# A SwiGLU block's down projection: 22 accumulating row blocks, or seven block products in sequence

## The reference

```python
x = x + rms_norm(mixed, g_post_mix)
h2 = rms_norm(x, g_pre_ffn)
ff = (jax.nn.silu(h2 @ w_gate) * (h2 @ w_up)) @ w_down
return x + rms_norm(ff, g_post_ffn)
```

## Time and profile before

| | us |
|---|---|
| median of 3 runs (605.81 to 607.92) | 607.17 |
| the profiled execution | 606.58 |
| its span, first to last instruction | 604.9 |
| TensorE busy | 589.1 (97%) |
| VectorE busy | 419.2 (69%) |
| ScalarE busy | 287.9 (48%) |
| GpSimd busy | 97.3 (16%) |

### The profile page before, as it was taken

How to read it: one execution, slowest core, us unless ns; L and a number is a source line. 1 busy time by engine, 2 the same in 40 slices (tenths; PEclk the granted TensorE clock), 3 DMA queues, 4 the chain that set the end, 5 groups by cost and what they waited for, 6 DMA issues and landing times.

```text
span 604.9 us, 9970 instructions
## 1 busy us (share of the span) xinstructions
PE 589.1 (97%) x3588; PEld 522.7 (86%) x3588; DVE 419.2 (69%) x704; ACT 287.9 (48%) x503; POOL 97.3 (16%) x98
## 2 busy tenths in 40 slices
PE   4999999999999999989999999999999999999996
PEld 4778888888888788989999999999999988888885
DVE  3768888787767955689887888788878632334433
ACT  6636665666535653545535353535353433224322
POOL 1111000010000000283332323232321100000000
PEclk9999999999999999999999999999999999999999
DMA  7644333333123550301313231323132473332111
GB/s 285 174 147 111 110 122 90 121 104 105 42 89 115 172 211 35 140 2 70 140 71 139 78 130 69 139 77 131 69 139 84 142 296 104 104 100 74 36 69 69
DMA packets 19540, 68.15 MB, mean 113 GB/s; under 512 B 2827, under 2 KB 2827, under 8 KB 19512
## 3 DMA queue, kind: packets, MB, share of 16 engines
q1 hardware_dynamic: 15944, 55.70, 26.4%
q0 software_dynamic: 3568, 12.09, 6.8%
HBM read 60.41 MB, written 4.22 MB: 107 GB/s over the span
## 4 chain that ended last, share of the span: by engine, by line
PE 91%; DVE 5%; ACT 1%; issue 1%; DMA 1%; SPq 0%; DVEq 0%; ACTq 0%
PE bank L1318 16%; PE bank L1320 16%; PE bank L1319 16%; PE bank L1568 11%; PE bank L1569 11%; PE bank L1570 11%; PE bank L1450 2%; PE bank L1438 2%; PE bank L1356 2%; PE bank L1422 1%; PE bank L1420 1%; DMA x_sb<-in_x 1%; DVE tok_lo L1228 1%; DVE form_lo L1152 1%; DVE mix_y L1130 1%
## 5 line engine op out<-in xcount | busy, mean ns | idle before, releaser
L1568 PE MATMUL bank<-tok_hi,form_hi 128*128 128x256 f32 x320 | 90.6, 283 | 0.4 <-DVE sp_v L1198 0.4
L1570 PE MATMUL bank<-tok_hi,form_lo 128*128 128x256 f32 x320 | 90.6, 283 | 0.0
L1569 PE MATMUL bank<-tok_lo,form_hi 128*128 128x256 f32 x320 | 90.6, 283 | 0.0
L889 DVE TENSOR_TENSOR w_lo<-raw,w_hi 128x1024 fp32r<-128x1024 f32 x46 | 55.7, 1218 | 43.0 <-ACT w_hi L574 42.9
L1318 PE MATMUL bank<-hn_hi,w_hi 128*128 128x512 f32 (+2 forms) x200 | 80.5, 403 | 0.0
L1320 PE MATMUL bank<-hn_hi,w_lo 128*128 128x512 f32 (+2 forms) x200 | 77.2, 386 | 0.0
L1319 PE MATMUL bank<-hn_lo,w_hi 128*128 128x512 f32 (+2 forms) x200 | 76.7, 384 | 0.0
L574 ACT CAST w_hi<-raw 128x1024 fp32r<-128x1024 f32 x46 | 47.9, 1046 | 48.1 <-PE bank L1320 45.6
L1569 PE MATMUL bank<-hn_lo,form_hi 128*128 128x256 f32 x240 | 67.9, 283 | 0.0
L1570 PE MATMUL bank<-hn_hi,form_lo 128*128 128x256 f32 x240 | 67.9, 283 | 0.0
L1568 PE MATMUL bank<-hn_hi,form_hi 128*128 128x256 f32 x240 | 67.9, 283 | 0.0
(11 more groups left out here) (195 smaller groups left out, 1329.6 us busy)
## 6 DMA issues: line engine op xcount, KB each, us to landing
raw<-in_w_in_units SPq DMA_DIRECT2D x24, 512.0 KB, 3.3
raw<-in_w_gate_units SPq DMA_DIRECT2D x22, 512.0 KB, 3.3
raw<-in_w_up_units SPq DMA_DIRECT2D x22, 512.0 KB, 4.2
raw<-in_w_down SPq DMA_DIRECT2D x22, 512.0 KB, 3.3
raw<-in_w_out SPq DMA_DIRECT2D x8, 512.0 KB, 3.3
q_lh<-q_hl POOLq DMA_DIRECT2D x12, 256.0 KB, 2.8
x_sb<-in_x SPq DMA_DIRECT2D x4, 512.0 KB, 5.1
x_rows<-x_sb POOLq DMA_DIRECT2D x4, 512.0 KB, 2.9
```

Source lines behind the costliest of these rows:

```text
L889: nc.vector.tensor_tensor(lo[:, :, :], raw[u % RAW][:, :, :], hi[:, :, :], ALU.subtract).then_inc(lo_done, 1)
L1568: nc.tensor.matmul(out_ap, sh, mh, start=first and k == 0, stop=False, skip_group_check=True)
L1569: nc.tensor.matmul(out_ap, sh, ml, start=False, stop=False, skip_group_check=True)
L1570: mm = nc.tensor.matmul(out_ap, sl, mh, start=False, stop=k == HK - 1, skip_group_check=True)
```

## The change

The down projection is done as seven products on 2 x 2 blocks as well. The activation is cut into two halves of features (11 blocks of 128 each) and two of tokens, `w_down` into two halves of rows and two of columns. Each of the seven products has 11 feature blocks x 2 token tiles x 3 matmuls of 512 columns. They run one after the other, with three pairs of PSUM banks (A, B, C) for the partial results.

The weight operand of a product is a block of `w_down` or a running sum of blocks. It is held in two places, `down_x` and `down_y` (22 KB a partition each), and its sums are made by transfers that add what they read to what lies in SBUF (`accum_op=ALU.add`), issued by GpSimd: block after block into `down_x` (products 1, 2 and 6) and `down_y` (product 4). SyncE loads `down_x` for product 0, `down_y` for product 3, and `down_y` again for product 5. Each of them comes in six groups of one or two row blocks (`DOWN_GROUPS`). The add of a group waits for the splitting of that group for the product that used it before.

The activation operand of products 0, 5 and 6 is a quarter of `act`; that of products 1 to 4 is a sum or difference of quarters in `down_s`, made by GpSimd in one instruction of 128 x 2816 numbers each (`down_sums`). ScalarE and VectorE split each operand whole (`down_form_hi`, `down_form_lo`, 128 x 2816) and the weights by groups (`down_hi`, `down_lo`) into four slots (`DSLOTS`); a slot is free when TensorE has finished the group four before. The join of partial results is done by ScalarE (`keep`, a copy out of PSUM) and VectorE (`join`). The norm at the end works on halves of a token tile. The diff, cut to this:

```diff
-LOOP_DOWN = 16
-LAST = FT - LOOP_DOWN
+DK = FT // 2
+DOWN_PRODUCTS = 7
+DOWN_GROUPS = ((3, 5), (5, 7), (7, 9), (9, 11), (0, 2), (2, 3))
+DG = len(DOWN_GROUPS)
+DOWN_SPLITS = DOWN_PRODUCTS * DG
+DSLOTS = 4
+DOWN_CHAIN = ((A_BANK, True), (C_BANK, True), (A_BANK, False), (C_BANK, False), (A_BANK, False), (B_BANK, True),
+              (A_BANK, False))
+DOWN_SOURCE = (("x", "in", 1), ("x", "added", 1), ("x", "added", 2), ("y", "in", 1), ("y", "added", 1), ("y", "in", 2),
+               ("x", "added", 3))
...
 @block.sync
+            for g in range(DG):
+                if g % 2 == 0 and g < 4:
+                    sp.wait_ge(form_lo_done, 4 * (SP_PAIRS - 1 + g // 2))
+                if g == 4:
+                    sp.wait_ge(prod, 7 * SP_PAIRS)
+                load_down("x", 0, 0, g)
+            for g in range(DG):
+                load_down("y", 1, 1, g)
+            for g in range(DG):
+                sp.wait_ge(dw_lo_done, DG * 4 + g + 1)
+                load_down("y", 1, 0, g)
...
 @block.gpsimd
             pool.wait_ge(act_done, FT)
             pool.dma_start(g_post_ffn_b[:, :], g_post_ffn.partition_broadcast(P)).then_inc(g_ffn_in, 16)
-            pool.wait_ge(prod, 7 * SP_PAIRS)
+            def add_down(which, f_half, n_half, n, g):
+                k0, k1 = DOWN_GROUPS[g]
+                dst = (down_x, down_y)[which == "y"]
+                pool.wait_ge(dw_lo_done, DG * n + g + 1)
+                pool.dma_start(dst[:, k0:k1, :], down_block(f_half, n_half, g), accum_op=ALU.add
+                               ).then_inc(down_added[which][g], 16)
+            def down_sums(n):
+                a11, a12 = act[:, 0:DK, 0:HALF], act[:, DK:FT, 0:HALF]
+                a21, a22 = act[:, 0:DK, HALF:SEQ], act[:, DK:FT, HALF:SEQ]
+                if n >= 2:
+                    pool.wait_ge(down_sum, n - 1)
+                    pool.wait_ge(da_lo_done, n)
+                else:
+                    pool.wait_ge(act_done, FT)
+                in0, in1, op = {1: (a21, a22, ALU.subtract), 2: (down_s[:, :, :], a11, ALU.subtract),
+                                3: (down_s[:, :, :], a12, ALU.add), 4: (a11, a21, ALU.subtract)}[n]
+                nc.gpsimd.tensor_tensor(down_s[:, :, :], in0, in1, op).then_inc(down_sum, 1)
+            down_sums(1)
+            for g in range(DG):
+                add_down("x", 0, 1, 0, g)
+            down_sums(2)
+            for g in range(DG):
+                add_down("x", 1, 1, 1, g)
+            down_sums(3)
+            for g in range(DG):
+                add_down("x", 1, 0, 2, g)
+            down_sums(4)
+            for g in range(DG):
+                add_down("y", 0, 1, 3, g)
+            pool.wait_ge(dw_lo_done, DG * 6)
...
 @block.scalar
+            def down_hi(s):
+                src, sem_in, count = down_raw(s)
+                act_e.wait_ge(sem_in, count)
+                if s >= DSLOTS:
+                    act_e.wait_ge(dw_used, s - DSLOTS + 1)
+                k0, k1 = DOWN_GROUPS[s % DG]
+                nc.scalar.copy(dw_hi[s % DSLOTS][:, 0:k1 - k0, :], src).then_inc(dw_hi_done, 1)
+            def down_form_hi(n):
+                if 1 <= n <= 4:
+                    act_e.wait_ge(down_sum, n)
+                if n >= 2:
+                    act_e.wait_ge(dw_used, DG * (n - 1))
+                nc.scalar.copy(da_hi[n % 2][:, :, :], down_form(n)).then_inc(da_hi_done, 1)
...
 turn(LAST_Q, ...), ScalarE
                     act_e.wait_ge(prod, 7 * LAST_Q)
-                    split(U_DOWN)
-                    split(U_DOWN + 1)
...
+                    down_form_hi(0)
                     act_e.wait_ge(form_lo_done, 4 * SP_PAIRS)
-                    for f in range(2):
-                        act_split(f, f)
+                    down_hi(0)
                 silu_first(q, par)
...
             silu_second(LAST_Q, LAST_Q % 2)
+            down_hi(1)
             act_e.wait_ge(prod, 7 * SP_PAIRS)
+            for s in range(2, DOWN_SPLITS):
+                down_hi(s)
+                if s % DG == 3 and s // DG + 1 < DOWN_PRODUCTS:
+                    down_form_hi(s // DG + 1)
+                if s in keep_at:
+                    keep(*keep_at[s])
...
 turn(LAST_Q, ...), VectorE
-                    split(U_DOWN)
-                    split(U_DOWN + 1)
                 if before:
                     product_of(q - 1, 1 - par)
                 sum_v6(q, par)
...
-                    act_split(0, 0, 1)
+                    down_form_lo(0)
                 sum_v67(q, par)
...
-                    act_split(1, 1, 2)
+                    down_lo(0)
                 up_second(q, par)
...
             gate_second(LAST_Q, LAST_Q % 2)
             product_of(LAST_Q, LAST_Q % 2)
+            down_lo(1)
+            for s in range(2, DOWN_SPLITS):
+                n, g = divmod(s, DG)
+                down_lo(s)
+                if g == 4:
+                    if n + 1 < DOWN_PRODUCTS:
+                        down_form_lo(n + 1)
+                    if n == 4:
+                        join(3, c12, True, ALU.subtract, 3)
+                    if n == 5:
+                        join(4, c22, False, ALU.subtract, 2)
+            join(5, c11, True, ALU.add, 1)
...
 @block.tensor
+            for n in range(DOWN_PRODUCTS):
+                pe.wait_ge(da_lo_done, n + 1)
+                if 2 <= n <= 4:
+                    pe.wait_ge(kept, n - 1)
...
+                if n == 6:
+                    pe.wait_ge(joined, 2)
+                for g in range(DG):
+                    if n == DOWN_PRODUCTS - 1 and g >= TAIL_GROUP:
+                        break
+                    pe.wait_ge(dw_lo_done, DG * n + g + 1)
+                    down_group(n, g, range(2)).then_inc(dw_used, 1)
+            for t in range(2):
+                for g in range(TAIL_GROUP, DG):
+                    if t == 0:
+                        pe.wait_ge(dw_lo_done, DG * (DOWN_PRODUCTS - 1) + g + 1)
+                    mm = down_group(DOWN_PRODUCTS - 1, g, (t,))
+                mm.then_inc(down_tile, 1)
```

More of the change, by code:

```diff
@@ L86 @@
 GU_BANKS = ((6, 7), (2, 3))
-DOWN_BANKS = (0, 4, 6, 2)
 STEPS = 8 * PAIRS
@@ L365, in norm_no, with down_block, down_raw, down_form @@
             return {SQ1: t + 1, SQ2: TT + 2 * t + 1, SQ3: TT + 2 * t + 2, SQ4: 3 * TT + t + 1}[n]
-        def nth(u):
-            return u + 1 if u < U_DOWN else u + 1 - 2 * SP_PAIRS
+        def down_block(f_half, n_half, g):
+            k0, k1 = DOWN_GROUPS[g]
+            return w_down[P * (DK * f_half + k0):P * (DK * f_half + k1),
+                          SEQ * n_half:SEQ * (n_half + 1)].rearrange("(k p) n -> p k n", p=P)
+        def down_raw(s):
+            n, g = divmod(s, DG)
+            which, by, count = DOWN_SOURCE[n]
+            k0, k1 = DOWN_GROUPS[g]
+            return ((down_x, down_y)[which == "y"][:, k0:k1, :], (down_in if by == "in" else down_added)[which][g],
+                    16 * count)
+        def down_form(n):
+            first, second = slice(0, HALF), slice(HALF, SEQ)
+            if n == 0:
+                return act[:, 0:DK, first]
+            if n == 5:
+                return act[:, DK:FT, first]
+            if n == 6:
+                return act[:, DK:FT, second]
+            return down_s[:, :, :]
         def raw_count(q):
@@ L883, in _ @@
+            act_e.wait_ge(joined, 3)
+            for t in range(2):
+                second_half(4 + t, t, 0, c11[:, t, :])
+            for t in range(2):
+                act_e.wait_ge(down_tile, t + 1)
+                second_half(6 + t, 2 + t, 0, bank[:, A_BANK + t, :])
         @block.vector
@@ L1614, in _ @@
                     pair(i * 2 + par, par)
-            def down(units, acts, t, first, last, halves=range(2)):
-                for h in halves:
-                    c = slice(4 * h, 4 * h + 4)
-                    mm = product(bank[:, DOWN_BANKS[t] + h, :],
-                                 (acts[0][:, P * t:P * (t + 1)], acts[1][:, P * t:P * (t + 1)]),
-                                 (units[0][:, c, :].rearrange("p k n -> p (k n)"),
-                                  units[1][:, c, :].rearrange("p k n -> p (k n)")), first, last)
-                return mm
@@ L1627, in _, with down_mm @@
[L1627 to L1637 removed]
+            def down_mm(n, k, slot, j, t, first, last):
+                b = DOWN_CHAIN[n][0]
+                (sh, sl), (mh, ml) = (da_hi[n % 2], da_lo[n % 2]), (dw_hi[slot], dw_lo[slot])
+                tokens_of = slice(P * t, P * (t + 1))
+                out_ap = bank[:, b + t, :]
+                nc.tensor.matmul(out_ap, sh[:, k, tokens_of], mh[:, j, :], start=first and DOWN_CHAIN[n][1],
+                                 stop=False, skip_group_check=True)
+                nc.tensor.matmul(out_ap, sh[:, k, tokens_of], ml[:, j, :], start=False, stop=False,
+                                 skip_group_check=True)
+                return nc.tensor.matmul(out_ap, sl[:, k, tokens_of], mh[:, j, :], start=False, stop=last,
```

(1 more changed line is left out.)

275 lines of the change are left out of this document (127 added, 148 removed).

## The result

| | before | after |
|---|---|---|
| median of the runs side by side | 606.71 (605.81 to 607.92) | 616.74 (608.73 to 617.79) |
| ratio, with its 95% interval | | 1.0134 [1.0084, 1.0184] |
| the profiled execution | 606.58 | 616.02 |
| its span | 604.9 | 614.3 |

The changed kernel is slower by 1.3%, where 604.8 us and a gain of 0.4% were forecast; 616.74 is inside the range of 600 to 632. Its own runs spread over 9 us, those of the kernel before over 2. Ten further runs of it (e0) had a median of 609.73, and all 14 together 612.1; so it is 2.5 to 10 us slower than the kernel before, depending on the set of runs, and none of the 14 reached the forecast (the fastest took 606.63).

A forecast was written before the change was run, and what follows sets the result against it. TensorE was taken as the bound, busy 97% of the span with nothing waiting. 15.0 us gained less 12.6 given back leaves 2.4: 607.17 to 604.8 us; 8-in-10 range 600 to 632.

The forecast's parts named there:

- The gain: Down projection: 462 matmuls in place of 528, 66 fewer at 0.2267 us each, saving 15.0 us.
- Parts 1 and 2: Last turn before the down projection loses 1.0 us; product 0 waits 0.3 us for group 1 and 4.8 for group 2.
- one or two us hang on the order of two engines: Product 0: if VectorE were just ahead of GpSimd, group 3 would be late, by some 3 us, instead of group 2.
- Part 3: Products 1, 2 and 3: a loop through GpSimd, ScalarE and VectorE outlasts TensorE's work, costing 3.6, 1.0 and 1.0 us.
- group 0 of the next product 1.14, which gets in before GpSimd's next sum: Products 1 to 3: VectorE's 1.14 us subtraction of the next product's group 0 precedes GpSimd's sum, which waits for group 5.
- The cycle: Each product with a sum: sum, casts and subtractions in a loop take 16.0 us with signalling, against TensorE's 14.96.
- Part 4: Weight transfers: only the last group of product 4 shows as waiting, 0.9 us, zero if adds are cheap.
- twice: Adding transfers cost twice a copy, both addends being read: 15.2 us an operand.
- 8 us of lead: Weight adds for a product are issued 8 us or more before ScalarE wants them.
- Part 5: Copies, joins and end: work lies in slack, steps behind the last matmul stay 5.5 us; cost 0, at most 1.
- The scaling of token tiles 0 and 1 has product 6 to hide it: Norm at the end: some 6 us of VectorE scaling fits within the 15 us of product 6.
- adding transfers too slow: Rival: below about 190 GB/s of added data an operand lands slower than 14.96 us; chance 0.42, two thirds above 615.

The follow-up runs named there:

- e6: Changed kernel with its 24 adding weight transfers made plain loads of the same number and size (output differs): 606.28 us, ratio 0.9996.
- e5: Changed kernel without the activation sums, products 1 to 4 taking plain quarters of `act` (output differs), adding transfers kept: 603.45 us, ratio 0.9944.
- e11: e9 with `down_y` loads waiting for product 2's splits and product 6's adds issued behind product 5's splits: 595.72 us, ratio 0.9806.
- e3: Changed kernel with 54 filler matmuls into an unused bank before TensorE's long waits, two semaphore waits moved to product 0: 613.57 us, ratio 1.0092.
- e7: Kernel before the change, with TensorE made to wait once in the tail for a GpSimd sum of 2048 numbers a partition: 613.48 us, ratio 1.0112.
- e2: Changed kernel with the norm's squares and the last join moved earlier, into product 6's loops: 610.58 us, ratio 0.9998.
- e9: Changed kernel with the edits of e1 and e2 together, transfers not moved: 598.54 us, ratio 0.9870.
- e1: Changed kernel with the four activation sums made by VectorE, not GpSimd: 602.28 us, ratio 0.9921.
- e4: Changed kernel with each GpSimd sum waiting until VectorE has done one more weight subtraction: 611.9 us, ratio 1.0083.
- e8: e9 with `down_y` loads waiting for product 1's splits and product 6's adds issued behind product 4's: 602.98 us, ratio 0.9945.
- e10: Changed kernel with each GpSimd sum cut into four instructions of 3, 3, 3 and 2 blocks: 617.40 us, ratio 1.0192.

## Why the prediction was wrong

Two steps turn the forecast gain of 2.4 us into a loss in the profiled execution: the waits were priced without the slower clock behind them (5.8 us), and the norm's work was held to be hidden (4.1 us). By parts:

**The gain** was right: 462 matmuls, 14.96 us a product.

**Parts 1 and 2** were right within 0.3 us. The long GpSimd instruction held VectorE whole, as rows 6 had shown for short ones, and a small fixed time plus a share proportional to size carried over from 1.29 to 6.55 us. That one or two us hang on the order of two engines was real, but at the start of product 1 and not in product 0: 1.5 us of waiting between e0's trace and the first one.

**Part 3** was right in product 1 (3.5 for 3.6) by luck, as another group was late for another reason, and too low by 3 us in products 2 and 3. The step that failed there is "group 0 of the next product 1.14, which gets in before GpSimd's next sum". In the profiled execution GpSimd got the ports first each time, so group 0 itself was held. The cycle had counted the cast of group 0 as ready; in product 1 it waited for the added weights and in product 2 for a slot. With plain loads (e6) it was ready, the order was the forecast one, and products 2 and 3 lost 0.7 us each (forecast 1.0). Product 1 lost 1.0 there, not 3.6; an estimate of the reason is the 2.7 us that half clock had cost TensorE in product 0 of e6, in which the weights caught up.

**Part 4**: "twice" was right (206 against 381 to 392 GB/s), its place was wrong. I let it cost 0.9 us in product 4; it cost nothing there and some 3.5 to 6 us in all (e6), by bringing group 0 so late that it met the sum, and it was the next limit once the sums were gone (e5). I had counted 8 us of lead for an add. Its landing took 9.8 us in the median, not the 3.3 of a lone load. Only part of that is `down_y`'s first load on the same engines, which I had named and not priced: with that load moved away (e11) the median is still 9.2, and with plain transfers (e6) it is 7.1.

**The clock** is the largest miss, 5.8 us, and no step of the prediction has it. Every wait in parts 2 and 3 was priced at its length alone. The page of the kernel before shows 1.00 throughout, because nothing there is idle; a change that brings idle stretches in leaves that state. e3 (idle time filled, no slow stretch) and e7 (idle time added to the old kernel, a slow stretch that cost 1.7 us) show it from both sides. The 5.8 us are where TensorE's time went, not what a full clock alone would give back: against e0's trace e3 won 1.7 of 3.5.

**Part 5** failed by 4.1 us: "The scaling of token tiles 0 and 1 has product 6 to hide it". The work fits in the time, but it stands behind the last cast on ScalarE's queue, and that waits for a slot, until 9 us before the last matmul. I had compared sizes and not walked the queue. e2 and e9 give 3.7 us back with order alone.

Together, clock and end, 9.9 of the 11.5 us between forecast and trace; products 2 and 3 are 3.0 more; part 4, part 1 and the earlier start gave 1.4 back. A rival had the right sign: adding transfers too slow, slower at 0.42. Its step, an operand that lands slower than a product runs, did not come about: 206 GB/s are above its limit of 190, and from product 4 on TensorE waits for nothing. But it is half right: the sign named for it, a cast that waits for an added transfer at a full DMA share, showed at the start of product 1. With no adding (e6) the kernel is as fast as the one before, so without the adds the loss is gone, but no gain is there either: the first sum's wait, the clock behind it and the longer end remain. With the sums moved and the adds in place (e1) it is faster than before.

**Open.** Why the runs of the unaltered change fall near 608 in some cases and near 616 in others is not settled: the two traces are of runs of 616.0 and 611.1 us, and none is of a run near 608. The granted clock over the span was 0.988 to 0.994 in the six runs up to 608.7 us and 0.984 to 0.987 in the six above 616, so slow stretches are part of it; that the order at the ports is the rest is argued from e0's trace and from the small spreads of e4 and e6. The 1.5 us wait in product 0 stayed in e9 and e11, and no run takes it apart.

## What to carry to other kernels

A wait brought into a matmul stream that had none costs its length and can cost the slower matmuls behind it: in e7 4.9 us of idle cost 6.7. An engine with free time isn't free if it shares ports with the one that feeds the bottleneck; the same sum was cheaper on the busier engine, 3.1 us for 6.6, and 14 subtractions beside the sums took 19 us less. A step said to be hidden has to be followed through the queue it stands in, and transfers moved to another time have to be laid beside those already there: e8 moved the collision, e11 removed it.

## What the runs showed of the hardware

In the down projection of all traces the granted TensorE clock went from its upper level (2.4 GHz) to the lower one (1.2 GHz) behind 14 idle stretches, each 2.1 to 4.9 us long, and stayed there for 3.4 or 6.8 us. Behind five others of 2.0 to 3.1 us (one in the changed kernel, two in e0, one each in e2 and e10) it stayed up, and so it did behind each of 1.9 us or less. What tells the five from the 14 no run here shows. Adding transfers moved 206 GB/s at a full share, plain ones of the same size 381 to 392 (e6); on GpSimd the issue of one took 1.2 us, of a plain one 0.72. A VectorE subtraction of 1.23 us that by the record began 0.15 us ahead of a GpSimd sum (498.40 and 498.55) still lasted until that was done, so a recorded start does not say who has the ports.
